# Loading an expert layer's dense weight units in pairs of 1 MB

## What is computed

```python
def peer_ffn(x, w_q, subkeys, u, v):       # u, v: 16384 experts x 1024, 64 MB each
    def block(xc):                         # 128 tokens
        q = (xc @ w_q).reshape(PEER_CHUNK, PEER_HEADS, 2, half)
        sc = jnp.einsum('thpd,hpnd->thpn', q, subkeys)
        s1, i1 = lax.top_k(sc[:, :, 0], PEER_TOPK)
        s2, i2 = lax.top_k(sc[:, :, 1], PEER_TOPK)
        ...                                # the best 16 of 16 x 16 pairs for each of 8 heads: idx, gate
        u_e = jnp.take(u, idx, axis=0)
        v_e = jnp.take(v, idx, axis=0)
        act = jax.nn.gelu(jnp.einsum('ted,td->te', u_e, xc))
        return jnp.einsum('te,ted->td', gate * act, v_e)
```

## Time and profile before

| | us |
|---|---|
| median of 3 runs (2087.05 to 2087.45) | 2087.44 |
| the profiled execution, whole | 2092.18 |
| its span | 2090.4 |
| TensorE busy | 2014.1 (96%) |
| VectorE busy | 1377.1 (66%) |
| ScalarE busy | 656.0 (31%) |
| GpSimd busy | 570.7 (27%) |
| mean granted TensorE clock | 0.986 of full |

### The profile page before, as it was taken

One profiled execution on the slowest core, in us unless ns is written; L12 is line 12 of the kernel. 1 busy time (PEld: TensorE's weight loads), 2 busy tenths in 40 slices (PEclk: granted clock), 3 DMA queues, 4 the chain that ended last, 5 costly groups with the idle time before them and its releaser, 6 DMA issues.

```text
span 2090.4 us, 32908 instructions
## 1 busy us (share of the span) xinstructions
PE 2014.1 (96%) x13084; PEld 1846.5 (88%) x13084; DVE 1377.1 (66%) x2724; ACT 656.0 (31%) x1331; POOL 570.7 (27%) x539
## 2 busy tenths in 40 slices
PE   9999999999999998979999999999998999999999
PEld 9877899999999887968689999999988898777887
DVE  7567589777754445248849987775554637977885
ACT  3455411344300000026631135430000105765554
POOL 1000103767653333000000376655342310000000
PEclk9999999999999999989999999999999999999999
DMA  7546489999999999724458999999999983343565
GB/s 261 191 132 213 149 298 354 401 409 396 394 400 409 409 409 409 295 73 152 139 178 264 357 396 409 408 402 408 409 409 406 409 327 125 106 136 128 188 191 169
DMA packets 169271, 612.40 MB, mean 293 GB/s; under 512 B 19984, under 2 KB 20096, under 8 KB 168864
## 3 DMA queue, kind: packets, MB, share of 16 engines
q1 hardware_dynamic: 107712, 391.63, 51.5%
q0 software_dynamic: 59984, 217.28, 26.5%
q10 hardware_dynamic: 1424, 1.41, 0.2%
HBM read 606.89 MB, written 1.05 MB: 291 GB/s over the span
## 4 chain that ended last, share of the span: by engine, by line
PE 68%; DMA 19%; DVE 9%; ACT 1%; issue 1%; POOL 1%; ACTq 0%; SPq 0%; POOLq 0%; DVEq 0%
PE ps L996 21%; PE ps L1027 14%; DMA plain<-in_peer_v 11%; PE ps L700 5%; DMA plain_in_xs<-in_peer_v 5%; PE ps L736 4%; PE ps L739 4%; PE ps L743 4%; PE ps L783 3%; PE ps L703 3%; PE ps L772 2%; PE ps L983 2%; PE ps L835 1%; DVE big L2360 1%; DVE big L2356 1%
## 5 line engine op out<-in xcount | busy, mean ns | idle before, releaser
L1027 PE MATMUL ps<-big,plain 128*128 128x160 f32 x2752 | 404.8, 305 | 20.2 <-DMA plain<-in_peer_v 16.5
L1027 PEld LDWEIGHTS ps<-big,plain 128*128 128x128 f32 x2752 | 383.7, 193 | 40.8 <-issue 20.6
L2533 DVE SCALAR_TENSOR_TENSOR big<-big 128x1024 f32<-128x1024 f32 x166 | 213.2, 1284 | 228.2 <-DMA big<-in_peer_v,big 223.4
L996 PE MATMUL ps<-big,plain 128*128 128x160 f32 x2496 | 356.6, 302 | 4.5 <-DMA plain<-in_peer_u 4.5
L996 PEld LDWEIGHTS ps<-big,plain 128*128 128x128 f32 x2496 | 345.1, 192 | 4.7 <-issue 4.7
L2113 DVE TENSOR_TENSOR lo<-raw,hi 128x1024 fp32r<-128x1024 f32 (+1 forms) x195 | 236.1, 1219 | 109.2 <-ACT hi L1506 108.4
L1506 ACT ACTIVATE hi<-raw 128x1024 fp32r<-128x1024 f32 (+1 forms) x195 | 204.8, 1055 | 154.5 <-PE ps L743 52.4
L3213 POOL DMA_INDIRECT big<-in_peer_v,big x168 | 165.9, 988 | 288.9 <-DVE big L2533 274.2
L996 PE MATMUL ps<-big,plain_in_xs 128*128 128x160 f32 x1600 | 233.3, 304 | 6.9 <-issue 6.9
L996 PEld LDWEIGHTS ps<-big,plain_in_xs 128*128 128x128 f32 x1600 | 223.9, 193 | 8.0 <-issue 8.0
L3213 POOL DMA_INDIRECT big<-in_peer_ur,big x132 | 168.9, 1279 | 152.2 <-DVE big L2527 121.0
(11 more groups left out here) (411 smaller groups left out, 2659.5 us busy)
## 6 DMA issues: line engine op xcount, KB each, us to landing
plain<-in_peer_v SPq DMA_DIRECT2D x172, 512.0 KB
plain<-in_peer_u SPq DMA_DIRECT2D x156, 512.0 KB
plain_in_xs<-in_peer_u SPq DMA_DIRECT2D x100, 512.0 KB
plain_in_xs<-in_peer_v SPq DMA_DIRECT2D x84, 512.0 KB
raw<-in_ret_vg SPq DMA_DIRECT2D x32, 512.0 KB
raw<-in_peer_q SPq DMA_DIRECT2D x24, 512.0 KB
raw<-in_ffn_up SPq DMA_DIRECT2D x22, 512.0 KB
raw<-in_ffn_down SPq DMA_DIRECT2D x22, 512.0 KB
```

What stands on the lines that cost most here:

```text
L996: ins = e.matmul(u.view[:, j * DENSE:(j + 1) * DENSE], w[:, k, :], Peer.xT[:, k, :], start=k == 0, stop=k == 7)
L1027: ins = e.matmul(us[b // 2].view[:, b % 2 * DENSE:(b % 2 + 1) * DENSE], w[:, b * 128:(b + 1) * 128], experts[:, k, :], start=k == 0 and b ...
L2533: e.scalar_tensor_tensor(out=sums, in0=rows, scalar=w, in1=sums, op0=ALU.mult, op1=ALU.add).then_inc(s_looked, 1)
```

## The change

Dense units are loaded in pairs. The host lays `peer_u` and `peer_v` out so that two units lie side by side in each partition's row; one DMA moves 128 rows of 8 KB, 1 MB. The ring has five places of a pair instead of ten of a unit, three of them in `plain` and two in `plain_in_xs`. A place is filled again when both of its units have been used. TensorE waits once for each pair, and takes the halves one after the other. The gathers of `peer_v` rows read a second, unpaired copy (`peer_vr`) of the same weights. The three ordinary loads stand after pairs 107, 110 and 112.

```diff
-N_PLAIN, N_FIRST, N_ROWS, IN_RAW, LATE = 10, 6, 9, 3, 6
-SLOTS = [[i % 10 for i in range(256)], [i % 10 if i < 210 else (i - 210) % 6 for i in range(256)]]
+N_PLAIN, N_FIRST, N_ROWS, IN_RAW, LATE = 5, 3, 9, 3, 6
+SLOTS = [[c % 5 for c in range(128)], [c % 5 if c < 105 else (c - 105) % 3 for c in range(128)]]
...
+        def unit_weights(l, i):
+
+            return plain[SLOTS[l][i // 2]][:, i % 2 * UNIT:(i % 2 + 1) * UNIT]
...
-                split_before[l, i] = max(n for n in in_ring[i % N_SPLIT] if n < end) if i < N_FIRST else end - 1
+                split_before[l, i] = max(n for h in range(2) for n in in_ring[(2 * i + h) % N_SPLIT] if n < end) \
+                    if i < N_FIRST else end - 1
...
-                        w = plain[SLOTS[l][2 * c + j]].rearrange("p (k n) -> p k n", k=8)
-                        e.wait_ge(*plain_landed(l, 2 * c + j))
+                        w = unit_weights(l, 2 * c + j).rearrange("p (k n) -> p k n", k=8)
+                        if j == 0:
+                            e.wait_ge(*plain_landed(l, c))
...
-                    e.wait_ge(*plain_landed(l, 128 + k))
+                    if k % 2 == 0:
+                        e.wait_ge(*plain_landed(l, 64 + k // 2))
...
-                table = A[f"peer_ur{l}"] if q < LISTS else A[f"peer_v{l}"].rearrange("n p d -> (n p) d")
+                table = A[f"peer_ur{l}"] if q < LISTS else A[f"peer_vr{l}"]
...
-                    e.wait_ge(*plain_used(l, max(n for n in range(i) if SLOTS[l][n] == SLOTS[l][i]) + 1))
-                src = A[f"peer_u{l}"][i] if i < 128 else A[f"peer_v{l}"][i - 128]
-                e.dma_start(plain[SLOTS[l][i]], src).then_inc(s_plain[SLOTS[l][i]], 16)
+                    e.wait_ge(*plain_used(l, 2 * max(n for n in range(c) if SLOTS[l][n] == slot) + 2))
+                src = A[f"peer_u{l}"][c] if c < 64 else A[f"peer_v{l}"][c - 64]
+                e.dma_start(plain[slot], src).then_inc(s_plain[slot], 16)
...
-                    if i in (215, 220, 225):
-                        if i == 215:
+                    if c in (107, 110, 112):
+                        if c == 107:
```

More of the change, by code:

```diff
@@ L271, in build @@
         hi, lo = sb("hi", [128, N_SPLIT, UNIT], F32R), sb("lo", [128, N_SPLIT, UNIT], F32R)
-        plain_a = nc.alloc_sbuf_tensor_at("plain", [128, N_FIRST, UNIT], F32, offset=split_at)
+        plain_a = nc.alloc_sbuf_tensor_at("plain", [128, N_FIRST, 2 * UNIT], F32, offset=split_at)
         lefts_at = (nc.sbuf_base + 31) // 32 * 32
@@ L280, in build @@
         xs = sb("xs", [128, 8, 2, S], F32R)
-        plain_b = nc.alloc_sbuf_tensor_at("plain_in_xs", [128, N_PLAIN - N_FIRST, UNIT], F32, offset=xs_at)
+        plain_b = nc.alloc_sbuf_tensor_at("plain_in_xs", [128, N_PLAIN - N_FIRST, 2 * UNIT], F32, offset=xs_at)
         plain = [plain_a[:, i, :] for i in range(N_FIRST)] + [plain_b[:, i, :] for i in range(N_PLAIN - N_FIRST)]
@@ L418, in pair_sums, with plain_landed @@
             return 6 * l + i + 1
-        def plain_landed(l, i):
-            slot = SLOTS[l][i]
-            return s_plain[slot], 16 * (l * SLOTS[0].count(slot) + SLOTS[l][:i + 1].count(slot))
+        def plain_landed(l, c):
+            slot = SLOTS[l][c]
+            return s_plain[slot], 16 * (l * SLOTS[0].count(slot) + SLOTS[l][:c + 1].count(slot))
+        def unit_weights(l, i):
+            return plain[SLOTS[l][i // 2]][:, i % 2 * UNIT:(i % 2 + 1) * UNIT]
         def plain_used(l, n):
@@ L648, in build @@
             for i in range(N_PLAIN):
-                split_before[l, i] = max(n for n in in_ring[i % N_SPLIT] if n < end) if i < N_FIRST else end - 1
+                split_before[l, i] = max(n for h in range(2) for n in in_ring[(2 * i + h) % N_SPLIT] if n < end) \
+                    if i < N_FIRST else end - 1
             for r in range(N_SPLIT):
                 n = min(n for n in in_ring[r] if n >= end)
-                i = max(i for i in range(256) if SLOTS[l][i] in (r, r + N_SPLIT))
-                W.after[n] = (*W.after.get(n, ()), (s_pused, 256 * l + i + 1))
+                c = max(c for c in range(128) if SLOTS[l][c] in (r // 2, (r + N_SPLIT) // 2))
+                W.after[n] = (*W.after.get(n, ()), (s_pused, 256 * l + 2 * c + 2))
         n = W.first["diff_k0"]
@@ L1024, in blocks @@
                 def blocks(k, first):
-                    w = plain[SLOTS[l][128 + k]]
+                    w = unit_weights(l, 128 + k)
                     for b in range(4 * first, 8 if first or k < 128 - LATE else 4):
@@ L3340, in sp @@
                     unit_load(n)
-                for i in range(256):
-                    plain_load(l, i)
-                    if i in (215, 220, 225):
-                        if i == 215:
+                for c in range(128):
+                    plain_load(l, c)
+                    if c in (107, 110, 112):
+                        if c == 107:
                             e.wait_ge(*looked(l, 126))
@@ L3440, in layouts @@
         a[f"peer_k{l}"] = v["peer_subkeys"][l].reshape(16, 128, 128).transpose(2, 0, 1).reshape(128, 2, 1024)
-        a[f"peer_u{l}"] = v["peer_u"][l].reshape(128, 128, 8, 128).transpose(0, 3, 2, 1).reshape(128, 128, 1024)
-        a[f"peer_ur{l}"], a[f"peer_v{l}"] = v["peer_u"][l], acc(v["peer_v"][l])
+        a[f"peer_u{l}"] = v["peer_u"][l].reshape(128, 128, 8, 128).transpose(0, 3, 2, 1)
+        a[f"peer_u{l}"] = a[f"peer_u{l}"].reshape(64, 2, 128, 1024).transpose(0, 2, 1, 3).reshape(64, 128, 2048)
+        a[f"peer_v{l}"] = v["peer_v"][l].reshape(64, 2, 128, 1024).transpose(0, 2, 1, 3).reshape(64, 128, 2048)
+        a[f"peer_ur{l}"], a[f"peer_vr{l}"] = v["peer_u"][l], v["peer_v"][l]
     a["ln_g"], a["ln_b"] = v["ln_g"], v["ln_b"]
```

7 lines of the change are left out of this document (4 added, 3 removed).

## The result

The changed kernel takes **2103.7 us** (median of 6 runs, 2101.83 to 2114.5), the kernel before beside it 2087.24 us: a ratio of **1.0082**, 95% interval 1.0054 to 1.0111, 16.5 us. That is a small change, but the interval lies clear of 1. The prediction, 2083 us with a range from 2072 to 2100, missed the sign and the range. The profiled run took 2109.9 us, 17.7 more than that of before.

The account below looks back on a forecast made before the run. TensorE bounds each pass's first half, a load the second. Terms -5.5 - 4 + 3 + 1 + 1.3 = -4.2 us from 2092.18 give 2088.0; the runs' median lies 4.7 lower, so 2083 us, range 2072 to 2100.

Parts of the forecast that it names:

- Packets and share: Second weights: 8 KB rows go as one packet, dense loads may take two thirds; TensorE's unit 2.17 us, not 2.56.
- The rival of even shares: 8 KB rows may be cut into 4 KB packets, pace staying 2.56 us per unit: +10.4, 2098 us; chance 0.22.
- Gathers left in layer 0: Second weights, layer 0: 18 or 19 gathers remain when TensorE arrives at the late blocks at 839.5 us.
- the tail's price: Remaining gathers before layer 0's late blocks, with nothing else loading: 1.5 us each, 28 us in all.
- The slow tail: Rival: busy VectorE blocks gather issue, 2.28 us each, in both layers' second weights: +17, 2105 us; chance 0.08.
- First pair: Start of each layer's first weights: first pair lands 3.0 us late plus 1 for slow start, layer 0; +1.3, layer 1.
- First weights "nothing": First weights: TensorE-bound, dense and look-up demands fit at 0.8 gather per unit, so no change in time.
- Layer 1: Second weights, layer 1: nothing won up to the transposes near 1626 us, late blocks 5 us earlier, clock costs 1: -4.
- a bound of +6 for layer 0: Second weights, layer 0: at 2.28 us per gather the late blocks start at 883 us, a loss of 6.
- TensorE's clock after the long wait: After idling before the late blocks TensorE starts slowly: 3 us added in layer 0, 1 in layer 1.

Follow-up runs that it names:

- `v8late`: Against the kernel before: 1 MB pairs with 8 KB rows in the second weights alone, except their first ten pairs, loaded singly in 4 KB rows; ratio 1.0031.
- `first1`: Against the kernel before: 1 MB pairs in 4 KB rows, but the first ten units of each layer loaded singly; ratio 1.0001, 2086.95 us.
- `mix3`: Against the kernel before: every third pair of the second weights as 1 MB with 8 KB rows, all else single 4 KB-row units; 1.0013, 2083.35 us.

## Why the prediction was wrong, by its own steps

**Packets and share: right.** q1 needs 70848 packets; TensorE runs at 2.17 us per unit without a wait for a dense load from 612 to 841 us; q1 moves 14.51 MB in 60 us (242 GB/s; I had said 240), q0 10.39 MB (173; I had said 165). TensorE has its 122 units at 841.4, where I had 839.5 from a stage that started 2.1 us earlier. The rival of even shares is dead.

**Gathers left in layer 0: the step that failed.** I had 18 or 19 left when TensorE arrives; it was 26. The wait was 40.29 us for 26 of them, 1.55 us each, against my 1.5, so the tail's price was right and only the count was not. (GpSimd issued the last 20 gathers 1.57 us apart, from 842.27 to 872.12. My reason for the low end, a VectorE that stands idle part of the time, was weak: it was busy 34.9 us of the 40.3.) The slow tail, the rival whose 2105 us is nearest, had the sum and not the mechanism: it needs 2.28 us each. I had counted steps of 3.12 us from look-up 97 at 601.8 on. It came at 612.10, 36.0 us after the stage's start instead of 27.7, and from it to the row of 840.72, 69 look-ups later, each took 3.31 us. The first takes some 3 look-ups off the count and the second 4, together about the whole error. Queues from 612 to 841 us:

```profile
q1 hardware_dynamic: 7996, 56.59, 59.6%
q0 software_dynamic: 10523, 38.19, 41.8%
```

q0 got 167 GB/s, where my 0.93 us in each 2.17 at 409 GB/s are 175, or 2.0 MB more. Two things had escaped me. The gathers slow down when the second weights' first loads go out, before look-up 97: in the first 28 us of the stage q0 moved 4.51 MB, against 5.19 before. And three units of `kv_w`, 1.57 MB, go out on q1 between pairs. While the queues were even they came out of q1's own half, and the dense units paid. Now TensorE's pace sets the dense units, and everything else on q1 comes on top, out of the gathers' share. Queues from 730 to 810 us, before and then after:

```profile
q1 hardware_dynamic: 4493, 16.35, 51.2%
q0 software_dynamic: 4492, 16.28, 51.2%
```

```profile
q1 hardware_dynamic: 3068, 20.71, 62.5%
q0 software_dynamic: 3423, 12.38, 38.8%
```

TensorE's pace needs 80 / 2.17 x 0.524 = 19.3 MB of q1 there, the rest, 1.4 MB, is about the three units of `kv_w`; q0 gets 12.38 MB instead of some 14.0 by my paces. The 0.7 MB ahead of look-up 97 and the 2.0 MB behind it, most of them in this window, are 5 gathers of 0.524 MB, of the 7 or 8 that the count was off. The other two or three are not found; `v8late`, with look-up 97 back in time, still had 24 left. That `kv_w` takes its bytes from the gathers is read from these two windows; no kernel was run with those units moved.

**First pair: mostly right.** Layer 0: +1.4 us at the first unit (I had +3.0), +3.2 at the key scores' consumer, 269.70 instead of 266.51; layer 1: +0.9 (+1.3). It was issued at 256.25, before I had it. Within one chip the pairs cost 1.0031, some 6.4 us, and `first1` shows all of it in the first filling: the size of my 5.3.

**First weights "nothing": wrong, its size open.** +2.7 us in layer 1, and in layer 0 of the kernel with 8 KB rows there alone 4.5 us more of waiting at the one-hot blocks. But kernels with the same first weights as before scatter by 4 us in layer 0 (307.0 with the copy, 311.0 in `mix3`), so single traces don't give the size. I had compared bytes (0.8 gather per unit fit) and not looked at who waits for VectorE in the meantime.

**Layer 1: the same error.** I had TensorE and VectorE meet at the transposes at 1626, 219 us after the stage's start; they met after 226.7 us (1644.34 less 1417.65, where the stage starts after the change). Look-up 97 there comes 6.3 us later than before, counted from the stage's start. I had also left out that GpSimd puts nine loads for a later stage (2.3 MB, the first of them `in_mem`) between the gathers there. VectorE stands behind them, before and then after:

```profile
1586.54 1.28 DVE L2533 SCALAR_TENSOR_TENSOR big<-big 128x1024 f32<-128x1024 f32 x1 [13.65 <-DMA big<-in_peer_v,big]
```

```profile
1622.78 6.84 DVE L2540 SCALAR_TENSOR_TENSOR big<-big 128x1024 f32<-128x1024 f32 x5 [16.81 <-DMA big<-in_peer_vr,big]
```

That is 3.2 us more of the delay. From the meeting on it took 79.3 us, where I had 77.5.

**The sum.** Second weights of layer 0: -5.5 forecast, +5.4 measured; layer 1: -4, +6.7; up to layer 0's second weights and at layer 1's first pair +5.3, +3.0; layer 1's first weights 0, +2.7. The first two, 21.6 us off, make the miss; the other two nearly cancel. The chances were set too kindly as well. I had a bound of +6 for layer 0 in hand, but tied it to GpSimd's issue alone, and carried the count of 18 or 19 into every case; no case had more gathers left.

## What to carry to other kernels

Where two queues keep the DMA engines full, a longer row is a bigger share and not more bandwidth: 409 against 416 GB/s, while 1.9 MB of each 25 changed sides. Before taking share for one queue, find how much slack the other one has at the point where both are needed. Here it was some 23 us; all pairs with long rows turned that into 40 us on the other side, and one pair in six left 5. When counting what the slower queue still gets, subtract everything that the favoured queue carries, not only the stream that you meant to favour. And load the first items of a ring singly: here that took back all of the 0.3% that pairs of 4 KB rows cost.

## What the runs showed of the hardware that I had not expected

Dense loads to 64 partitions each, in place of all 128, made the whole kernel take 28% (4 KB rows) and 32% (8 KB rows) longer, with the DMA row at 9 as before, but at about 270 and 250 GB/s instead of 409. Why the engines are slower on such transfers no run here shows. The Trainium skill (DMA: Bandwidth & Descriptors, rules for kernel authors) advises one transfer over 128 partitions in place of two halves; the runs agree with the advice and put a price on it.

TensorE's clock after the long wait: the windows of the changed kernel (us, busy, granted clock, DMA share, GB/s) while it stood before the late blocks, and just behind:

```profile
842.00:882.00 40.00, 0.30 (x1) 0.54 0.83 307
882.00:890.00 8.00, 8.00 (x27) 0.74 0.19 66
```

It is granted 0.54 of full speed in the idle stretch, close to the lower of its two levels, and the eight records of the late blocks take 5.93 us instead of 3.60. That price, 2.3 us, was near the 3 us of the prediction for layer 0; in layer 1 it was 2.9 us (6.53 instead of 3.60), where I had 1.
